# Accumulating one token tile's gates in DRAM by indirect DMAs, beside a shorter one-hot stage

## The reference

```python
q = (x_c @ w_q).reshape(PEER_CHUNK, PEER_HEADS, PEER_QDIM)         # 8 heads
s1 = jnp.einsum('chd,nd->chn', q[..., :half], sub_k1)              # 128 keys
s2 = jnp.einsum('chd,nd->chn', q[..., half:], sub_k2)              # 128 keys
t1, i1 = lax.top_k(s1, PEER_TOPK); t2, i2 = lax.top_k(s2, PEER_TOPK)   # 16 each
...
top_s, pos = lax.top_k(cand_s, PEER_TOPK)                          # 16 of 256 pairs
ids = jnp.take_along_axis(cand_i, pos, axis=-1)                    # i1 * 128 + i2
gate = jax.nn.softmax(top_s, axis=-1)
hid = jax.nn.gelu(jnp.einsum('chkd,cd->chk', u[ids], x_c), approximate=False)
return jnp.einsum('chk,chkd->cd', (gate * hid), v[ids])
```

## Time and profile before

| | us |
|---|---|
| median of three runs | 1973.86 |
| the profiled execution, its own time | 1973.14 |
| its span in the profile | 1971.3 |
| retrieval, from the first queries to the end of the block | 686 to 1224 |
| gate stage | 1224 to 1435 |
| experts | 1435 to 1971 |

### The profile page before, as it was taken

The page is one execution under the profiler, slowest core; times in us unless marked ns, Lnnn a source line. Parts: engine busy times, 40 slices in busy tenths (PEclk is TensorE's granted clock), DMA queues, the critical chain, the costliest instruction groups (busy, mean ns, idle before and its releaser), DMA issues. The chain is left out here.

```text
span 1971.3 us, 35045 instructions
## 1 busy us (share of the span) xinstructions
PE 1896.8 (96%) x13809; PEld 1657.6 (84%) x13809; DVE 1477.1 (75%) x3142; ACT 756.0 (38%) x1165; POOL 362.0 (18%) x337
## 2 busy tenths in 40 slices
PE   8999999899999899999999998999789999999999
PEld 8999887677854689999999998998668888888887
DVE  5353335766662369999999999999878888888887
ACT  5322445222240234433443343776433333333332
POOL 2001100011100003213331330000433222322221
PEclk9999999999999999999999999999999999999999
DMA  4222101100040348668867974287789999999996
GB/s 160 86 87 74 44 22 65 56 3 3 3 172 32 132 132 328 241 235 331 312 236 256 345 278 144 87 268 217 253 336 361 338 337 338 349 337 338 338 339 249
DMA packets 176116, 407.25 MB, mean 207 GB/s; under 512 B 16848, under 2 KB 100048, under 8 KB 175312
## 3 DMA queue, kind: packets, MB, share of 16 engines
q1 hardware_dynamic: 133040, 255.96, 37.9%
q0 software_dynamic: 39744, 144.72, 19.4%
q10 hardware_dynamic: 3168, 4.33, 0.6%
HBM read 358.77 MB, written 46.14 MB: 205 GB/s over the span
## 5 line engine op out<-in xcount | busy, mean ns | idle before, releaser
L89 PE MATMUL eo_ps<-vh,e_wh 128*128 128x512 f32 x768 | 300.3, 391 | 8.7 <-DVE e_wl L2062 8.7
L90 PE MATMUL eo_ps<-vh,e_wl 128*128 128x512 f32 x768 | 299.7, 390 | 0.0
L91 PE MATMUL eo_ps<-vl,e_wh 128*128 128x512 f32 x768 | 299.7, 390 | 0.0
L2028 POOL DMA_INDIRECT e_rows<-in_v,gidx x128 | 140.3, 1096 | 386.3 <-DVE e_acc_t L2042 352.7
L1651 POOL DMA_INDIRECT g_stage<-in_u_rows,gidx x112 | 135.5, 1210 | 391.4 <-DVE gidx L1746 236.8
L2011 ACT CAST vh<-vraw 128x1024 fp32r<-128x1024 f32 x96 | 100.7, 1049 | 235.2 <-PE eo_ps L91 230.2
L89 PE MATMUL h_ps<-x2h,h_uh 128*128 128x384 f32 x520 | 181.2, 348 | 8.4 <-DVE h_ul L1507 5.3
L89 PEld LDWEIGHTS eo_ps<-vh,e_wh 128*128 128x128 f32 x768 | 144.8, 189 | 40.2 <-DVE vl L2053 5.6
L1503 ACT ACTIVATE h_hid<-h_ps 128x384 f32<-128x384 f32 x128 | 63.5, 496 | 290.6 <-PE h_ps L91 209.5
L91 PE MATMUL h_ps<-x2l,h_uh 128*128 128x384 f32 x520 | 174.9, 336 | 0.0
L89 PE MATMUL h_ps<-x2h,q_uh 128*128 128x384 f32 x504 | 170.6, 339 | 4.5 <-ACT h_hid L1503 4.5
(11 more groups left out here) (318 smaller groups left out, 4304.0 us busy)
## 6 DMA issues: line engine op xcount, KB each, us to landing
vraw<-in_v SPq DMA_DIRECT2D x96, 512.0 KB, 6.2
g_stage<-in_u SPq DMA_DIRECT2D x63, 512.0 KB, 6.6
h_uraw<-in_u SPq DMA_DIRECT2D x45, 512.0 KB, 5.4
wraw<-in_w_z SPq DMA_DIRECT2D x43, 512.0 KB, 3.5
HID_scratch<-h_hid SPq DMA_DIRECT2D x106, 192.0 KB, 4.0
e_hid<-HID_scratch SPq DMA_DIRECT2D x96, 192.0 KB, 6.6
G_scratch<-g_stage SPq DMA_DIRECT2D x16, 1024.0 KB, 12.0
g_hot<-in_v SPq DMA_DIRECT2D x32, 512.0 KB, 6.3
```

The lines of the kernel that those rows point to most:

```text
L89: nc.tensor.matmul(out, a[0], b[0], start=start, stop=False)
L90: nc.tensor.matmul(out, a[1], b[0], start=False, stop=False)
L91: return nc.tensor.matmul(out, a[0], b[1], start=False, stop=stop)
L2028: nc.gpsimd.indirect_dma_start(rows[:, j % GBUF_E], None, d["v"].rearrange("c p n -> (c p) n"), bass.IndirectOffsetOnAxis(ap=gidx[:, j:j + ...
```

## The change

Three tiles are still dense, but only tiles 2 and 1 go through the one-hot steps, in that order (`ONEHOT = (2, 1)`), 64 steps. Tile 2 stays in SBUF, tile 1 is stored in 8 parts with a semaphore for each. Tile 0's part of G is cleared in the recurrence's block by 8 DMAs from SP out of a tile of zeros. Its gates are added in DRAM by Pool: for each pick one indirect DMA with `compute_op=ALU.add` writes 128 elements of 4 bytes, one per token, to the places (i1 x 128 + i2) x 256 + token. Each waits until the one before has landed. Heads 0 to 6 are added in the retrieval, behind and between the gathers; the last head's in the gate stage.

In the gate stage the chunks of u are spread by eighths (`FILL`): 8 eighths before the first step, then 3, 3, 2 in turn for the first 32 steps, 2, 1, 1, 1 for the others, and the remaining 42 after the steps. The last head's gathers go to the start of the stage and its dots between steps 4 and 30. SP issues tile 1's 8 stores after the last step and then loads G[0] behind them; in the experts, `acc_t` and Pool's first gather of v wait for all 8 parts. The retrieval begins with two more splits and two gelus ahead of the first head (`AHEAD`). The semaphores that are cleared for new use are more and are cleared one block earlier.

```diff
@@ rwkv_recurrence, SP and DVE @@
+            sp.wait_ge(zeroed, 1)
+            for r in range(GPARTS):
+                a = slice(r * NK // GPARTS, (r + 1) * NK // GPARTS)
+                sp.dma_start(keep["G"][a, :, 0:P].rearrange("a b t -> b a t"),
+                             zeros[:].unsqueeze(1).broadcast_to([P, NK // GPARTS, P])).then_inc(keep["g_cleared"], 16)
...
+            nc.vector.memset(zeros[:], 0.0).then_inc(zeroed, 1)
@@ place_gates @@
+    places = keep["G"].rearrange("a b (t o) -> (a b t) o", o=1)
+    def scatter(pool, j, weights):
+        if j > 0:
+            pool.wait_ge(keep["g_added"], j * 16)
+        nc.gpsimd.indirect_dma_start(
+            places, bass.IndirectOffsetOnAxis(ap=keep["place"][:, j:j + 1], axis=0), weights, None,
+            compute_op=ALU.add).then_inc(keep["g_added"], 16)
@@ peer_retrieval, ACT @@
+            for m in range(AHEAD):
+                split_hi(act, m + 2)
+                gelu(act, m)
...
-                    if m >= 1:
+                    if m > AHEAD:
                         gelu(act, m - 1)
-                    split_hi(act, m + 2)
+                    if m >= AHEAD:
+                        split_hi(act, m + 2)
@@ peer_retrieval, Pool @@
+            pool.wait_ge(keep["g_cleared"], GPARTS * 16)
+            for h in range(PH - 1):
+                pool.wait_ge(row_listed, h + 1)
+                for k in range(GBUF_R):
+                    gather(h * TOPK + k)
+                pool.wait_ge(listed, h + 1)
+                for k in range(TOPK):
+                    keep["scatter"](pool, h * TOPK + k, picks[:, 2, 0, h, k:k + 1])
+                    if k + GBUF_R < TOPK:
+                        gather(h * TOPK + k + GBUF_R)
@@ peer_retrieval, DVE @@
+            for m in range(AHEAD):
+                split_lo(dve, m + 2)
...
-                nc.vector.scalar_tensor_tensor(out=gidx[:, h * TOPK:h * TOPK + TOPK], in0=picks[:, 0, ND, h],
-                                               scalar=float(NK), in1=picks[:, 1, ND, h], op0=ALU.mult,
-                                               op1=ALU.add).then_inc(row_listed, 1)
+                link(nc.vector.scalar_tensor_tensor(out=expert[:], in0=picks[:, 0, :, h], scalar=float(NK),
+                                                    in1=picks[:, 1, :, h], op0=ALU.mult, op1=ALU.add))
+                picked = slice(h * TOPK, h * TOPK + TOPK)
+                link(nc.vector.scalar_tensor_tensor(out=place[:, picked], in0=expert[:, 0], scalar=float(2 * P),
+                                                    in1=token[:].broadcast_to([P, TOPK]), op0=ALU.mult, op1=ALU.add))
+                nc.vector.tensor_copy(gidx[:, picked], expert[:, ND]).then_inc(row_listed, 1)
@@ gate_matrix @@
-    STEPS = ND * NS
+    STEPS = len(ONEHOT) * NS
+    FILL = ((3, 3, 2), (2, 1, 1, 1))
+    quota = [FILL[n // NS][n % len(FILL[n // NS])] for n in range(STEPS)]
+    dot_step = [4 + j * 7 // 4 for j in range(TOPK)]
@@ gate_matrix, SP @@
+            sp.wait_ge(staged, STEPS)
+            for r in range(GPARTS):
+                a = slice(r * QA, (r + 1) * QA)
+                sp.dma_start(G[a, :, P:2 * P].rearrange("a b t -> b a t"), second[:, a]).then_inc(keep["g_part"][r], 16)
+                if r == 0:
+                    sp.dma_start(first["v"], d["v"][0]).then_inc(keep["e_v_in"][0], 16)
+                    sp.wait_ge(keep["hid_stored"][0], 16)
+                    sp.dma_start(first["hid"], keep["HID"][0]).then_inc(keep["e_g_in"][0], 16)
+            sp.wait_ge(keep["g_added"], PH * TOPK * 16)
+            sp.wait_ge(keep["g_part"][0], 16)
             sp.dma_start(first["g"], G[0]).then_inc(keep["e_g_in"][0], 16)
@@ gate_matrix, Pool @@
+            for j in itertools.islice(gathers, 2):
+                gather(j)
+            for m in range(NRC + GSLOT, NCHUNK):
                 load(pool, m)
+                for j in itertools.islice(gathers, 3):
+                    gather(j)
+                if m >= NRC + GSLOT + 5:
+                    for k in itertools.islice(scatters, 2):
+                        keep["scatter"](pool, LATE + k, keep["last_gate"][:, k:k + 1])
+            pool.wait_ge(keep["g_added"], PH * TOPK * 16)
@@ gate_matrix, DVE @@
+                for j in range(TOPK):
+                    if dot_step[j] == n:
+                        dve.wait_ge(rows_in[j], 16)
+                        nc.vector.tensor_tensor_reduce(rows[:, j], rows[:, j], x2t[:], 1.0, 0.0, ALU.mult, ALU.add,
+                                                       hdot[:, LATE + j:LATE + j + 1]).then_inc(dotted, 1)
@@ experts, SP and Pool @@
+                    for r in range(GPARTS):
+                        sp.wait_ge(keep["g_part"][r], 16)
                     sp.dma_start(acc_t[:], keep["H2"][:, ND]).then_inc(acc_in, 16)
...
             pool.wait_ge(v_hi, 2)
+            for r in range(GPARTS):
+                pool.wait_ge(keep["g_part"][r], 16)
```

More of the change, by code:

```diff
@@ L1254, in _ @@
                 sp.dma_start(keep["H2"][:, i], acc[:, i]).then_inc(keep["h2_stored"], 16)
+        @block.gpsimd
+        def _(pool):
+            for n in keep["spent"]:
+                pool.sem_clear(range(n, n + 1))
         @block.tensor
@@ L1821, in gate_matrix @@
     NS = P // TB
-    STEPS = ND * NS
-    BESIDE = 17
-    TAIL = NRC + BESIDE
-    QA = NK // 8
+    STEPS = len(ONEHOT) * NS
+    QA = NK // GPARTS
     NBANK = 4
     LATE = (PH - 1) * TOPK
+    REST = NCHUNK - NRC
+    FILL = ((3, 3, 2), (2, 1, 1, 1))
+    quota = [FILL[n // NS][n % len(FILL[n // NS])] for n in range(STEPS)]
+    step_of = [-1] * KD + [n for n in range(STEPS) for _ in range(quota[n])]
+    step_of = (step_of + [STEPS] * (REST * KD))[0:REST * KD]
+    begins = [step_of[i * KD] for i in range(REST)]
+    ends = [step_of[i * KD + KD - 1] for i in range(REST)]
+    dot_step = [4 + j * 7 // 4 for j in range(TOPK)]
     with ExitStack() as ctx:
@@ L1851, in _ @@
         def _(sp):
-            for tile in range(ND - 1):
-                sp.wait_ge(staged, NS * (tile + 1))
-                for r in range(8):
-                    a = slice(r * QA, (r + 1) * QA)
-                    sp.dma_start(G[a, :, tile * P:tile * P + P].rearrange("a b t -> b a t"),
-                                 stage[tile][:, a]).then_inc(g_stored[tile], 16)
-            for b in range(2):
-                sp.wait_ge(g_stored[b], 8 * 16)
-            sp.wait_ge(placed, STEPS)
-            sp.dma_start(first["v"], d["v"][0]).then_inc(keep["e_v_in"][0], 16)
+            sp.wait_ge(staged, STEPS)
@@ L1915, in _ @@
                 mm.then_inc(placed, 1)
-            for m in range(TAIL, NCHUNK):
-                product(pe, m)
+            fill(STEPS)
         @block.scalar
         def _(act):
+            split_hi(act, NRC + 1)
             for n in range(STEPS):
                 tile, i = n // NS, n % NS
-                if n % 4 == 0 and n // 4 <= BESIDE:
-                    split_hi(act, NRC + n // 4)
-                if tile == 2 and i == 0:
-                    act.wait_ge(g_stored[0], 8 * 16)
+                if n in begins[0:REST - 1]:
+                    split_hi(act, NRC + begins.index(n) + 1)
+                if tile == 1 and i == 0:
+                    act.wait_ge(dotted, TOPK)
                 act.wait_ge(placed, n + 1)
-                nc.scalar.copy(stage[tile % 2][:, :, i * TB:i * TB + TB].rearrange("p a t -> p t a"),
+                nc.scalar.copy(stage[tile][:, :, i * TB:i * TB + TB].rearrange("p a t -> p t a"),
                                ps[:, n % NBANK]).then_inc(staged, 1)
-                if n % 4 == 1 and 2 <= n // 4 <= BESIDE + 1:
-                    gelu(act, NRC + n // 4 - 2)
-                    store(act, NRC + n // 4 - 2)
-            for m in range(TAIL, NCHUNK):
-                if m + 1 < NCHUNK:
-                    split_hi(act, m + 1)
-                gelu(act, m)
-                store(act, m)
+                if n in ends or n == 0:
+                    gelu(act, NRC + (ends.index(n) if n > 0 else 0))
+                    store(act, NRC + (ends.index(n) if n > 0 else 0))
+            for i in range(REST):
+                if begins[i] == STEPS and i + 1 < REST:
+                    split_hi(act, NRC + i + 1)
+                if ends[i] == STEPS:
+                    gelu(act, NRC + i)
+                    store(act, NRC + i)
 def experts(nc, d, keep):
@@ L2125, in build @@
                 keep["x2t"] = ctx.enter_context(nc.sbuf_tensor("x2t", [P, D], F32))
+                keep["g_cleared"], keep["g_added"] = (ctx.enter_context(nc.semaphore(n)) for n in ("g_cleared", "g_added"))
+                keep["g_part"] = [ctx.enter_context(nc.semaphore(f"g_part{r}")) for r in range(GPARTS)]
                 keep["h2_stored"] = ctx.enter_context(nc.semaphore("h2_stored"))
```

105 lines of the change are left out of this document (61 added, 44 removed).

## The result

The changed kernel takes **2120.46 us** (median of four runs, 2112.24 to 2129.86) against 1974.01 before on the same chip: a ratio of 1.074, 95% interval 1.069 to 1.079. The forecast of 2021 had the sign, and the mechanism of one of the two losses (the chain of scatters); the other, in the one-hot stage, it had as a gain of 22 us. Its range ended at 2105. The profiled run took 2119.83 us, with a span of 2117.9.

The account below looks back on a forecast made before the run. PE was taken as busy 96% of the span, with DVE the bound in the one-hot stage. Retrieval end 1293.8 + 192 to the experts + 533.0 experts + 1.8 = 2021 us; own range 1979 to 2084, full range 1944 to 2105.

Parts of the forecast that it names:

- Start of the retrieval: Retrieval start: two splits and gelus ahead of head 0 remove chunk 2's 4.5 us wait, -4.4 us.
- Lists: Retrieval: two more small DVE operations per head, showing 0.2 us a head and 0.45 in the last, +1.7 us.
- Clearing: Recurrence: clearing G by 8 stores of 1 MB from SP, where SP issues nothing else, costs 0.
- Scatters: Retrieval, Pool: sixteen chained scatters a head for seven heads delay the block's end to 1293.8, +72 us.
- r: Pool's scatters: time from one landing to the next, taken as 4.0 us, bounds 3.3 and 5.
- P: Retrieval: Pool's period per head with the scatter chain, 78.4 us where the head has 67.1.
- rival D: Pool's scatters: slower round trips, r 4.6 and more, time 2084 at 4.6; chance 0.12.
- the signs: Expected in the profile, among others: DVE waits of 8 to 11 us at dot 0 per head.
- One-hot stage: One-hot steps: DVE's work sums to 146.5 us, the last step copied some 154.5 us from the stage's start.
- Rival E: One-hot stage doesn't shrink: chunk loads behind gathers stall some 20 us; 2050, or 1978 if chain hides (chance 0.03).
- Store and start of the experts: After the last step: store, G[0] and remaining products take 37.5 us; experts start 192 us after the stage, -22 us.
- Break-even: Retrieval: the change neither gains nor loses at a head period of 71.6 us, r = 3.55.

Follow-up runs that it names:

- the kernel with both edits: Changed kernel with a head's scatters waiting only for the head before and the splits two steps later: 1949.08 us against 1973.52 before the change.
- Experiment 5: Changed kernel with scatters waiting only for the head before and splits two steps later: 1949.08 us; the same with `AHEAD = 0`: 1956.74 us.

## Why the prediction missed, step by step

1. **Start of the retrieval: right in kind, gain larger.** The 4.5 us wait went as said, and the first gather comes 5.4 us sooner behind the first product of the queries than before the change. In after this is hidden by a start of that product that lies 4.5 us later, within what it varies from run to run.
2. **Lists: hidden in after, small where they show.** Nothing waits for a list in after. With the chain out of the way a head takes 67.6 us for 67.15 before: 0.4 and not the 0.2 forecast, if the lists are it.
3. **Clearing: no cost that can be seen.** One kernel with all of it starts the queries where before does (675.5 and 675.2).
4. **Scatters: the mechanism held, the term r was mis-sized.** P was to be 78.4 and is 83.2 in head 1 and 84.0 on the mean of the seven. The first landing was near 17 in head 1, better than 20; a quiet round trip is 3.2, better than 3.95. But the mean is 4.7 and not 4.0, since I took r from rows of single DMAs and put the traffic into the first landing alone. Each of the sixteen turns meets the same loads and gathers. Pool's time for one is also 1.59 us and not the 1.18 of a gather, and up to 2.4 with a gather beside it. By its r this is rival D, from 4.6 up, but not by its time: with the first landing sooner the retrieval alone would have made 2021 into some 2060 and not D's 2084. D had a chance of 0.12, while the landings in the earlier trace rows (4.5 to 12.8 us for gathers of one size) said that the spread lay upward. DVE's wait at dot 0 is 18.8 us in head 1 and 15.3 in a later head, where the signs had 8 to 11.
   The Trainium skill's 2.0 us fixed per DMA (page and section as in the prediction) gave an estimated r of 2.8. Quiet plain writes come 2.4 apart and quiet adding ones 3.2, so it is about right where little else moves; the page has no price for adding, and that section's fixed cost has no term for the other traffic that makes 4.7 here.
5. **One-hot stage: the sum of DVE's work was right, the step failed.** That sum, 146.5 us, is what the traces have over the 64 steps: 145.6 in after, 143.6 with the later split. (The text's terms add up to 154.8 with it, not to 154.5.) But the sum was made as if DVE never waits; after waits 51.0 us, and the steps take 206.1. A split in DVE's order waits for ACT, ACT for PE, and PE for DVE's matrices. Before the change ACT's `split_hi` stood ahead of a step and DVE's `split_lo` behind the third step after it, and from 1224 to 1404 the trace of before has no such wait at all; the change puts both at the same step. It came up 16 times, 3.2 us each. The code showed both places; I counted the split among the durations and not among the waits. Rival E had the stage not shrinking for another reason, loads behind gathers. Only one load was late, by 8.8 us of ACT's time, and by 8.5 with the later split, where the stage has its length. That this length agrees with the 192 forecast is in part luck: in the kernel with both edits the steps take 149.8 for 154.5, and from there to the experts it is 41.7 for 37.5.
6. **Store and start of the experts: 41.8 for 37.5.** SP issues the seven later parts in 28.5 us, from 1548.4 on, and starts the load of G[0] at 1577.0, 32 us after the last copy, where I had 28.8. The stores are as priced; the loads of v and of the hidden values, which stand behind the first part in SP's order, take 2.9 us of SP's time and had no price. `acc_t` and Pool's row gathers cost nothing that can be told apart.
7. **Break-even.** It was put at P = 71.6 with the stage at 192. Experiment 5 stands on its good side and has both terms as worked out (67.5 us a head, 192 the stage). Two terms of the forecast were too small together, by 39.4 and 51.6 us; the range took in a miss of one at a time.

## What to carry to other kernels

A chain of small DMAs that each wait for the one before costs its landings under the traffic of the place, times their number, and idle time of the engine that issues them is not by itself room for it; ask first whether each link protects the same bytes, since loosening it to one wait a head was worth 119 us, all that the scatters cost. On an engine that works in order, place an operation that waits for others where its input is already there: two steps later was worth 52 to 55 us at the same work. A stage's length is its bound engine's sum only if that engine is shown to wait for nobody.

## What the hardware showed that was not expected

An adding scatter of 128 elements takes Pool 1.59 us and 144 packets, a plain one 1.00 us and 32. Its landing ranged from 2.9 to 13.9 us in one kernel. With DVE's waits gone the granted clock over the 64 steps was 0.98, in place of 0.86, and the same products kept PE busy 139.9 us in place of 160.2. Of the 55 us by which the steps got shorter 51.0 are the waits that went, so the clock gave little on top of them; how much of the waits themselves came from the lower clock, since DVE waited there for PE's products, was not told apart.
